# Hybrid block on one core: a seventh weight chunk joins the step-wise first stage, and each next modulation product moves inside the present step's matmuls

## What is computed

```python
cond = jax.nn.silu(c)
mod = cond @ w_ada[layer] + b_ada[layer]                  # 2048 x 12288
shift1, scale1, gate1, shift2, scale2, gate2 = split(mod, 6)
h = x * (1.0 + scale1) + shift1
proj = h @ w_in                                           # sb_q, sb_k, sb_v, hg_q, ...
# stick-breaking attention, 8 heads of 128, per block of queries
z = einsum('bhqd,bhkd->bhqk', q, k) * scale
log_1mb = where(mask, log_sigmoid(-z), 0.0)
tail = cumsum(log_1mb, axis=3, reverse=True) - log_1mb
w = where(mask, exp(log_sigmoid(z) + tail), 0.0)
a_out = einsum('bhqk,bhkd->bhqd', w, v)
```

## Time and profile before

| | us |
|---|---|
| Median of three runs (lowest, highest) | 2281.61 (2278.86, 2285.75) |
| The profiled execution | 2278.52 |
| Its span, first to last instruction | 2276.9 |
| PE busy, share of the span | 1937.7, 85% |
| DVE busy | 1365.1, 60% |
| ACT busy | 390.6, 17% |
| First stage's last matmuls end | 138.6 |
| First scores | 152.2 |

### The profile page before, as it was taken

How to read it: one execution, slowest core, us unless ns; L and a number is a source line. 1 busy time by engine, 2 the same in 40 slices (tenths; PEclk the granted TensorE clock), 3 DMA queues, 4 the chain that set the end, 5 groups by cost and what they waited for, 6 DMA issues and landing times.

```text
span 2276.9 us, 27806 instructions
## 1 busy us (share of the span) xinstructions
PE 1937.7 (85%) x10646; PEld 1309.3 (58%) x10646; DVE 1365.1 (60%) x2008; ACT 390.6 (17%) x1001; POOL 782.8 (34%) x554
## 2 busy tenths in 40 slices
PE   4899899998999999989888888888975888897455
PEld 4788688887888888878654545555640222221001
DVE  7821378776444441246798889777876444444664
ACT  0112212211000001021232212544530000000011
POOL 1000000000000000004365546767878644554783
PEclk9999899999999999999899899888985999999556
DMA  9963366575576656318899999999999999999997
GB/s 391 428 276 143 116 270 246 216 292 197 234 284 245 230 212 259 140 69 331 311 383 414 405 408 414 398 402 398 392 406 371 417 417 410 399 413 354 364 365 270
DMA packets 104603, 722.41 MB, mean 317 GB/s; under 512 B 29740, under 2 KB 29740, under 8 KB 32060
## 3 DMA queue, kind: packets, MB, share of 16 engines
q0 software_dynamic: 78800, 466.66, 51.9%
q1 hardware_dynamic: 25696, 254.35, 28.0%
HBM read 858.35 MB, written 4.19 MB: 379 GB/s over the span
## 4 chain that ended last, share of the span: by engine, by line
PE 43%; DMA 29%; DVE 12%; issue 8%; POOL 5%; ACT 2%; POOLq 0%; DVEq 0%; SPq 0%; ACTq 0%
PE ps L777 21%; DMA arena<-expert_u,expert 14%; DMA arena<-expert_v,expert_q 11%; PE ps L785 10%; POOL arena L489 4%; PE ps L801 3%; PE ps L974 3%; DVE work L1410 2%; PE ps L1002 2%; DMA mod_rows<-expert_u,expert 2%; DVE mod_rows L1167 1%; PE ps L1048 1%; DMA mod_rows<-expert_v,expert_q 1%; DVE work L1223 1%; DVE work L1130 1%
## 5 line engine op out<-in xcount | busy, mean ns | idle before, releaser
L1410 DVE CUSTOM_DVE_ANT_0 work<-arena,buf_b 128x2048 f32<-128x2048 f32 x166 | 380.8, 2294 | 265.5 <-DMA arena<-expert_u,expert 232.1
L974 PE MATMUL ps<-arena,mod_rows 128*32 128x512 f32 x1640 | 270.5, 740 | 197.1 <-DMA arena<-expert_v,expert_q 166.0
L777 PE MATMUL ps<-buf_a,arena 128*128 128x256 f32 x1920 | 424.2, 383 | 6.1 <-DVE arena L1241 5.3
L777 PEld LDWEIGHTS ps<-buf_a,arena 128*128 128x128 f32 x1920 | 367.5, 192 | 57.2 <-issue 6.7
L489 POOL DMA_INDIRECT arena<-expert_v,expert_q x205 | 339.8, 1658 | 159.1 <-PE ps L974 97.1
L489 POOL DMA_INDIRECT arena<-expert_u,expert x205 | 266.1, 1298 | 239.8 <-DVE work L1410 124.2
L476 POOL DMA_DIRECT2D arena<-ada_late x32 | 16.9, 529 | 770.9 <-DVE mod_rows L1167 642.7
L1002 PE MATMUL ps<-arena 128*128 128x256 f32 x1024 | 273.3, 418 | 4.2 <-DMA arena<-dense_u 4.2
L1002 PEld LDWEIGHTS ps<-arena 128*128 128x128 f32 x1024 | 202.8, 207 | 128.8 <-issue 94.8
L974 PEld LDWEIGHTS ps<-arena,mod_rows 128*32 128x32 f32 x1640 | 37.2, 118 | 333.2 <-DMA arena<-expert_v,expert_q 270.3
L653 ACT ACTIVATE work<-work 32x4 f32<-32x4 f32 (+3 forms) x320 | 66.4, 207 | 551.3 <-DVE work L1410 543.8
(11 more groups left out here) (244 smaller groups left out, 2083.1 us busy)
## 6 DMA issues: line engine op xcount, KB each, us to landing
arena<-weights SPq DMA_DIRECT2D x62, 2048.0 KB, 8.0
arena<-ada_late POOLq DMA_DIRECT2D x32, 2048.0 KB, 9.4
arena<-ada_early SPq DMA_DIRECT2D x16, 2048.0 KB, 17.7
arena<-dense_u SPq DMA_DIRECT2D x32, 1024.0 KB
arena<-expert_v SPq DMA_DIRECT2D x32, 1024.0 KB
arena<-w_early SPq DMA_DIRECT2D x8, 1536.0 KB, 9.8
arena<-expert_u,expert POOLq DMA_INDIRECT x205
arena<-expert_v,expert_q POOLq DMA_INDIRECT x205
```

The lines of the kernel that those rows point to most:

```text
L777: last = mm(ps[:, bank, c * TOKENS:(c + 1) * TOKENS], ring[slot][:, first + k, c * P:(c + 1) * P], rhs[:, k, :], start=(k == 0), stop=(k = ...
L974: last = mm(ps[j * GROUP:(j + 1) * GROUP, n // HEADS * QUADS + g, :], spread_w[n % 2][:, e, :], v_slot[row % V_RING][:, j * QCOLS:(j + 1) ...
L1410: v.tensor_tensor_reduce(out=products[n > 2], in0=u_slot[s], in1=h2[:, n // HEADS], scale=1.0, scalar=0.0, op0=ALU.mult, op1=ALU.add, accu ...
```

## The change

A seventh chunk, sb_v[0], joins the six whose columns accumulate in the first stage. The weight tile of a step has 1792 columns times 2 instead of 1536 times 2 (`EARLY_COLS`), and behind the 12 column tiles of each row tile PE makes two matmuls for the values, one for each block of 128 tokens, into bank 6. The products of the modulation share bank 7, with four columns for even and four for odd steps (`MOD_BANK`). The product of step g + 1 stands in the middle of the second row tile of step g, with six column tiles and two value matmuls behind it. In the second stage the first value projection is gone, the others are moved one place forward in halves, and the values' banks and slots are numbered anew.

```diff
+EARLY_COLS = (EARLY_PAIRS * 2 + 1) * COLS
-V_BANKS, V_SLOTS, V_TURNS = (7, 2, 2, 2), (0, 1, 2, 2), (0, 0, 0, 1)
+V_BANKS, V_SLOTS, V_TURNS = (6, 0, 2, 2), (None, 1, 2, 2), (None, 0, 0, 1)
+MOD_BANK = 7
...
-        F_HGRN = tuple(n + m * 2 for n, m in zip(F_ATTN, (1, 1, 1, 0)))
+        F_HGRN = tuple(n + m for n, m in zip(F_ATTN, (1, 2, 2, 0)))
...
-            stream(2, ATTN0, range(3), F_ATTN)
+            for s in (1, 2):
+                sp.wait_ge(used[s], 1 + F_ATTN[s])
+                sp.dma_start(arena[:, s * CHUNK:(s + 1) * CHUNK], weights[(ATTN0 + s - 1) * P:(ATTN0 + s) * P, :]).then_inc(loaded[s], 16)
+            stream(1, ATTN0 + 2, range(3), (F_ATTN[0], F_ATTN[1] + 1, F_ATTN[2] + 1))
...
             pe.wait_ge(s_ones, 1)
-            for g in range(EARLY_STEPS):
+            def mods(g):
+
                 pe.wait_ge(used[(2 * g + 1) % 4], 2 + (2 * g + 1) // 4)
                 for j in range(4):
-                    last = mm(ps[:, 6 + g % 2, j:j + 1], mod_sum[g % 2][:, j * P:(j + 1) * P], one_col, start=True, stop=True)
+                    last = mm(ps[:, MOD_BANK, 4 * (g % 2) + j:4 * (g % 2) + j + 1], mod_sum[g % 2][:, j * P:(j + 1) * P], one_col, start=True, stop=True)
                 last.then_inc(s_mod, 1)
+
+            mods(0)
+            for g in range(EARLY_STEPS):
                 pe.wait_ge(early_loaded[g % 2], (g // 2 + 1) * 16)
                 for k in range(2):
                     pe.wait_ge(s_h, 2 * g + k + 1)
                     for c in range(EARLY_TILES):
+                        if k == 1 and c == EARLY_TILES // 2 and g < EARLY_STEPS - 1:
+                            mods(g + 1)
...
+                    for b in range(BLOCKS):
+                        last = mm(ps[:, V_BANKS[0], b * COLS:(b + 1) * COLS], h_t[:, 2 * g + k, b * P:(b + 1) * P],
+                                  early_slot[g % 2][:, k, EARLY_TILES * P:EARLY_COLS], start=first and b == 0, stop=end, skip_group_check=True)
...
-            pe.wait_ge(loaded[0], (F_ATTN[0] + 1) * 16)
-            project_rows(V_BANKS[0], 0, h_t, [0])
-            project_rows(V_BANKS[0], 0, h_t, [1]).then_inc(used[0], 1)
+            pe.wait_ge(s_q, 1)
+            pe.wait_ge(loaded[1], (F_ATTN[1] + 1) * 16)
+            project_rows(V_BANKS[1], 1, h_t, [0])
             pe.wait_ge(s_const, 16)
             pe.wait_ge(s_q, EARLY_PAIRS)
             pe.wait_ge(s_k, EARLY_PAIRS)
             scores(0)
-            pe.wait_ge(loaded[1], (F_ATTN[1] + 1) * 16)
-            project_rows(V_BANKS[1], 1, h_t, [0])
+            project_rows(V_BANKS[1], 1, h_t, [1]).then_inc(used[1], 1)
+            pe.wait_ge(s_v, 1)
             tails(0)
-            project_rows(V_BANKS[1], 1, h_t, [1]).then_inc(used[1], 1)
+            pe.wait_ge(loaded[2], (F_ATTN[2] + 1) * 16)
+            project_rows(V_BANKS[2], 2, h_t, [0])
             attend(0)
             scores(1)
...
```

More of the change, by code:

```diff
@@ L65 @@
 EARLY_TILES = EARLY_PAIRS * 2 * COLS // P
+EARLY_COLS = (EARLY_PAIRS * 2 + 1) * COLS
 EARLY_STEPS = KT // 2
 MOD_COLS = 4 * P
-V_BANKS, V_SLOTS, V_TURNS = (7, 2, 2, 2), (0, 1, 2, 2), (0, 0, 0, 1)
+V_BANKS, V_SLOTS, V_TURNS = (6, 0, 2, 2), (None, 1, 2, 2), (None, 0, 0, 1)
+MOD_BANK = 7
 ATTN0 = 0
-HGRN0 = ATTN0 + PAIRS + 2
+HGRN0 = ATTN0 + PAIRS + 1
 GATE0 = HGRN0 + 4 * PAIRS
@@ L163, in block_kernel @@
         ada_slot = [arena[:, (4 + s) * CHUNK:(5 + s) * CHUNK] for s in range(2)]
-        early_slot = [arena[:, (4 + s) * CHUNK:(4 + s) * CHUNK + 2 * EARLY_TILES * P].rearrange("p (k n) -> p k n", k=2) for s in range(2)]
+        early_slot = [arena[:, (4 + s) * CHUNK:(4 + s) * CHUNK + 2 * EARLY_COLS].rearrange("p (k n) -> p k n", k=2) for s in range(2)]
         branch_in = arena[:, 6 * CHUNK:7 * CHUNK].rearrange("p (a k t) -> p a k t", a=2, k=BRANCH_KT)
@@ L538, in _ @@
                 for k in range(2 * g, 2 * g + 2):
-                    me.step(run(shift1[:, k:k + 1], ps[:, 6 + g % 2, k % 2:k % 2 + 1], ACT.Identity, bias=shift1_bias[:, k:k + 1]))
-                    me.step(run(scale1[:, k:k + 1], ps[:, 6 + g % 2, 2 + k % 2:3 + k % 2], ACT.Identity, bias=scale1_bias[:, k:k + 1]))
+                    me.step(run(shift1[:, k:k + 1], ps[:, MOD_BANK, 4 * (g % 2) + k % 2:4 * (g % 2) + k % 2 + 1], ACT.Identity, bias=shift1_bias[:, k:k + 1]))
+                    me.step(run(scale1[:, k:k + 1], ps[:, MOD_BANK, 4 * (g % 2) + 2 + k % 2:4 * (g % 2) + 3 + k % 2], ACT.Identity, bias=scale1_bias[:, k:k + 1]))
                 me.settle()
@@ L549, in v_copy @@
             def v_copy(pair):
-                act_e.wait_ge(used[V_SLOTS[pair]], 1 + F_ATTN[V_SLOTS[pair]] + V_TURNS[pair] + 1)
+                if pair:
+                    act_e.wait_ge(used[V_SLOTS[pair]], 1 + F_ATTN[V_SLOTS[pair]] + V_TURNS[pair] + 1)
                 run(v_rows, ps[:, V_BANKS[pair], :].rearrange("p (b n) -> p b n", b=2), ACT.Copy).then_inc(s_v, 1)
@@ L566, in _ @@
                 if pair == EARLY_PAIRS - 1:
-                    act_e.wait_ge(used[0], 1 + F_ATTN[0] + 2)
+                    act_e.wait_ge(used[0], 1 + F_ATTN[0] + 1)
                     q_copy(EARLY_PAIRS, 0)
@@ L839, in _ @@
             scores(0)
-            pe.wait_ge(loaded[1], (F_ATTN[1] + 1) * 16)
-            project_rows(V_BANKS[1], 1, h_t, [0])
+            project_rows(V_BANKS[1], 1, h_t, [1]).then_inc(used[1], 1)
+            pe.wait_ge(s_v, 1)
             tails(0)
-            project_rows(V_BANKS[1], 1, h_t, [1]).then_inc(used[1], 1)
+            pe.wait_ge(loaded[2], (F_ATTN[2] + 1) * 16)
+            project_rows(V_BANKS[2], 2, h_t, [0])
             attend(0)
             scores(1)
-            pe.wait_ge(loaded[2], (F_ATTN[2] + 1) * 16)
+            project_rows(V_BANKS[2], 2, h_t, [1]).then_inc(used[2], 1)
+            tails(1)
+            pe.wait_ge(loaded[0], (F_ATTN[0] + 1) * 16)
             pe.wait_ge(s_v, 2)
-            project_rows(V_BANKS[2], 2, h_t, [0])
-            tails(1)
-            project_rows(V_BANKS[2], 2, h_t, [1]).then_inc(used[2], 1)
+            project_t(0, 0, h_t, halves=[0])
             attend(1)
             scores(2)
-            pe.wait_ge(loaded[0], (F_ATTN[0] + 2) * 16)
-            project_t(0, 0, h_t, halves=[0])
+            project_t(0, 0, h_t, halves=[1]).then_inc(used[0], 1)
             tails(2)
-            project_t(0, 0, h_t, halves=[1]).then_inc(used[0], 1)
+            pe.wait_ge(loaded[1], (F_ATTN[1] + 2) * 16)
+            project_t(1, 1, h_t, halves=[0])
             attend(2)
-            pe.wait_ge(loaded[1], (F_ATTN[1] + 2) * 16)
-            project_t(1, 1, h_t).then_inc(used[1], 1)
+            project_t(1, 1, h_t, halves=[1]).then_inc(used[1], 1)
             pe.wait_ge(loaded[2], (F_ATTN[2] + 2) * 16)
@@ L1578 @@
     sb_q, sb_k, sb_v, hg_q, hg_f, hg_i, hg_g = (w[n * PAIRS:(n + 1) * PAIRS] for n in range(7))
-    early = np.stack([sb_q[:EARLY_PAIRS], sb_k[:EARLY_PAIRS]], axis=1).reshape(EARLY_PAIRS * 2, P, EARLY_STEPS, 2, COLS)
-    attention = np.stack([sb_v[0], sb_v[1], sb_v[2], sb_q[3], sb_k[3], sb_v[3]])
+    early = np.concatenate([np.stack([sb_q[:EARLY_PAIRS], sb_k[:EARLY_PAIRS]], axis=1).reshape(EARLY_PAIRS * 2, P, CHUNK), sb_v[:1]])
+    early = early.reshape(EARLY_PAIRS * 2 + 1, P, EARLY_STEPS, 2, COLS)
+    attention = np.stack([sb_v[1], sb_v[2], sb_q[3], sb_k[3], sb_v[3]])
     ada = f32(w_ada)[0]
@@ L1600 @@
         "bias_late": f32(b_ada)[:, ADA_COLS:],
-        "w_early": early.transpose(2, 1, 3, 0, 4).reshape(EARLY_STEPS * P, 4 * EARLY_TILES * P // 2),
+        "w_early": early.transpose(2, 1, 3, 0, 4).reshape(EARLY_STEPS * P, 2 * EARLY_COLS),
         "weights": weights.reshape(N_CHUNKS * P, CHUNK),
```

## The result

The changed kernel takes 2288.8 us, the median of 18 runs from 2285.2 to 2299.7, against 2283.7 us of the kernel before in 18 runs. The ratio is 1.0025 with an interval of 1.0016 to 1.0033: slower by some 5 us, where I had forecast 3.5 us faster. The time lies outside the stated range of 2272 to 2287. The forecast stood on 2281.6 us for the kernel before, the median of three runs; over 18 runs it is 2.1 us higher.

A forecast was written before the change was run, and what follows sets the result against it. Transfer was taken to bound the first stage until the last sum at 124.2, PE from there. Terms: -6.4, +1.7 for the queue, +1.2 for the clock, sum -3.5: 2278.1 us against 2281.6; range 2272 to 2287.

The forecast's parts named there:

- The transfer's size: First stage: weight tile grows by 0.262 MB, seven ahead of the last step add 4.3 us; last sum ends at 128.5.
- the projection's removal: Second stage: the first value projection leaves, -13.8 us; ScalarE's 1.5 us also leave PE's path.
- the later order: After the scores: each half projection still covers the softmax work; cost 0, at most one microsecond per pair.
- The first query copy: Before the scores: the next value projection waits for this copy, whose bank it writes; 0.5 us.
- PE's own 28 matmuls: End of the first stage, after the last product: 28 matmuls take 12.2 us.
- Moved, the release of the weight buffers: First-stage steps: weight tiles are issued 4.5 us after the sum, so the queue runs dry briefly; +1.7 us, bounds 0 and 5.5.
- By its own sign the term: Stated test of the queue term: it is wrong if the DMA share dips in every step or in none.
- Its parts, 0.6 and 1.0: Dry queue in the first stage: 0.6 us in all over some steps, 1.0 us in the first step.
- The clock, +1.2: First-stage steps: PE's stop and narrow products lower the granted clock, 0.7 of a 1.7 us fall on the path; bounds 0 and 11.9.
- 1 us of slack: Third step of the first stage: its longer PE stop may lower the clock, but the step has 1 us to spare.
- By its own sign this term: Stated test of the clock term: it is wrong if windows at 0.5 follow the products in more than two steps.
- My rival with the clock: Middle of each step: clock falls, late release, dry queue, late sum, self-sustaining; 11.9 us instead of 1.2, +7.2, 2288.8; chance 0.15.

The follow-up runs named there:

- the first experiment: Changed kernel with SP's queue rewoven from the third step: next step's first modulation tile issued before the weight tile, second behind; 2273.8 us, 0.9955 of the kernel before.

## Why the prediction was wrong

**The transfer's size, the projection's removal, the later order: right.** Steps between dry spells are 14.1 us apart, as in the first experiment. The scores follow with one half projection before them, and 83.7 us for the rest of attention equal the 83.8 of before. The first query copy holds PE for 0.69 us where I had 0.5. PE's own 28 matmuls take 12.1 us.

**"Moved, the release of the weight buffers", +1.7: the step that failed.** I had 4.5 us from sum to release, 2.6 of start and completion with 9.2 of transfer, that is 11.8, from release to the next sum's start, and 12.3 for the sum: 28.6 for two steps against 28.2. Measured are 6.4, 12.4 and 12.3: 31.1. Of the 2.5 us too few in each pair, 0.6 are the restart of the queue, which I had from a single transfer into an idle queue, and 1.9 are the fallen clock between product and release. There were two such pairs and a first step. In the first, I had the release at 49.0; it came at 50.75, since the product (1.87 us) and the eight matmuls ran at half the clock throughout, and the start that hangs on it came at 63.1, where 49.0 + 11.8 is 60.8. This term and the clock's together put 2.9 us ahead of the last sum; they measured 9.1 (137.6 against the 128.5 of the transfer alone). By its own sign the term was not wrong, for the share dipped neither in every step nor in none; it was its size that failed. (Its parts, 0.6 and 1.0, add up to 1.6, not 1.7.)

**The clock, +1.2: mis-sized, since I priced it beside the loop and not in it.** I gave the third step 1 us of slack. It has none: a dry queue makes the sum late, so PE waits 3.1 us instead of 1.0, so the clock falls, so the release is 1.9 us later, and the queue dries further. By its own sign this term was wrong: slow matmuls follow four of the products. My rival with the clock described the loop and had the sign. Its number, 2288.8, is the measured one by luck: it counts seven falls of 1.7 us from 2281.6, where there were four, and the kernel before takes 2283.7 over 18 runs. It had the wrong period, for it takes only every second step (in the others PE arrives after the sum and does not stop: product at 90.2, sum at 89.5), and only a part of the lever: with the queue rewoven the loop is gone although the clock still falls in places, while the clock held up by fillers left 1.2 to 1.3 us of dry queue in a step. The chance of 0.15 that I gave it was too low, with the fall after 2.6 us without wide matmuls on record, and a third fall that I did not count: the matmuls from 72.95 us on in the kernel before took 12.02 us, behind 3.1 us without wide ones.

**The sum.** To the last sum 131.4 was forecast, if all of the clock's term is put ahead of it (128.5 + 1.7 + 1.2), and 137.6 measured, 6.2 more. Behind it 19.1 instead of 17.3, 1.8 more, for the last fall. Together 8.0, which turns -3.5 into +4.5 at the scores.

**What the pages had made of it.** The trace has 12.4 us for 3.93 MB behind a dry queue, 3.2 above the 9.2 of the transfer. The Trainium skill (DMA: Bandwidth & Descriptors, "Anatomy of one DMA") states 2.0 us of fixed cost, for transfers issued from GpSimd. With it the release term would have been smaller still, so for this queue the measurement decides.

The granted clock was 0.50 behind each stop of 3 us. The Trainium skill (TensorE: Matmul & The Clock Gate, "A second HAM failure mode: psum-queue depth-cycling") tells of a kernel whose short idles between groups of matmuls make the clock oscillate; this trace agrees, with falls behind four such stops. The first experiment bounds it: stops of 0.7 to 0.8 us in its last three steps left the clock at 1.00.

**Open.** Why in some steps 0.3 to 0.7 MB more go through before the awaited tile has landed, and in others none; and how the 3 us of restart divide between a start that moves only 143 to 315 GB/s and the completion.

## What to carry to other kernels

When work moves behind a wait, look first at what is queued behind that work's own signal: here the gain in PE's list was lost on SP's, where two urgent tiles stood behind one that was not. Two buffers that wait on each other across two engines form a loop; add up its whole period, with the clock at its low level where an engine stops in it, and compare it with the bound. A margin of tenths of a microsecond in such a loop is no margin: reorder the queue so that nothing urgent waits for the late signal.

## What the runs showed of the hardware

A queue that has run dry comes back slowly: 172, 143 and 315 GB/s in the three microseconds from 82 us on, and the share of busy time does not show it (1.02 at 172 GB/s). From the release to the sum that needs the tile behind it, 3.93 MB in all, it took 12.3 to 12.5 us three times in the changed kernel. A long step need not be a dry one: with fillers in the first step only, the step from 89.69 to 105.52 took 15.8 us at 423 GB/s, 6.70 MB where its tiles hold 6.03.

The granted clock fell in a step whose stop was filled with four wide matmuls as well (0.62 from 104 to 108 us), with 1.6 us of stop left. The length of the stop alone does not decide: with fillers in the first step only, PE stopped for 2.28 us ahead of the product at 72.4 and the clock stayed at 1.00, and for 2.29 us ahead of the one at 102.0 and it fell to 0.50.
